# Two changes in the mixer of a two-layer decoder step: the prompt softmax works on scores that stay in PSUM, and the mixer's end runs in another order

## The reference, cut to what matters

```python
a = u @ w_in
y_c = silu(layernorm(depthwise_conv(a_conv))) @ pw      # 2 of the 8 row blocks of w_out
y_p = (window means - x) @ pool_w * pool_scale          # 2 blocks
y_a = sparse_attend(q, selected keys, selected values)  # 4 blocks
y = jnp.concatenate([y_c, y_p, y_a], axis=-1) @ w_out
```

```python
s = jnp.einsum('btngd,btknd->btngk', qg, ks) * HEAD_DIM ** -0.5
s = jnp.where(valid, s, -jnp.inf)
p = jax.nn.softmax(s, axis=-1)
o = jnp.einsum('btngk,btknd->btngd', p, vs)
```

## Time and profile before

| | us |
|---|---|
| median of 3 runs (lowest, highest) | 1151.5 (1150.71, 1151.86) |
| the profiled execution: its time | 1149.91 |
| its span in the trace | 1148.3 |
| busy: PE, DVE, ACT, GpSimd | 1082.8, 741.7, 514.2, 190.1 |

### The profile page before, as it was taken

How to read it: one execution, slowest core, us unless ns; L and a number is a source line. 1 busy time by engine, 2 the same in 40 slices (tenths; PEclk the granted TensorE clock), 3 DMA queues, 4 the chain that set the end, 5 groups by cost and what they waited for, 6 DMA issues and landing times.

```text
span 1148.3 us, 27626 instructions
## 1 busy us (share of the span) xinstructions
PE 1082.8 (94%) x9358; PEld 1025.1 (89%) x9358; DVE 741.7 (65%) x1211; ACT 514.2 (45%) x832; POOL 190.1 (17%) x241
## 2 busy tenths in 40 slices
PE   6999999999779999999999999999986799999996
PEld 6999999888448999999999999998863699999996
DVE  5676744788955766764476776448888466676544
ACT  5544433621444644443464444345215455444432
POOL 4211100411300311110041111004222022111001
PEclk9999999999879999999999999999998899999998
DMA  8464565343536355555435465563444445555541
GB/s 279 163 231 165 199 234 189 138 139 131 151 94 178 129 183 183 181 185 178 154 110 206 172 217 202 193 224 124 123 137 138 93 139 184 182 180 177 189 149 38
DMA packets 90465, 191.17 MB, mean 166 GB/s; under 512 B 12323, under 2 KB 48483, under 8 KB 90403
## 3 DMA queue, kind: packets, MB, share of 16 engines
q1 hardware_dynamic: 87426, 184.82, 48.7%
q0 software_dynamic: 2976, 5.53, 2.0%
HBM read 187.71 MB, written 2.59 MB: 166 GB/s over the span
## 4 chain that ended last, share of the span: by engine, by line
PE 85%; DVE 5%; ACT 3%; SPq 2%; issue 2%; DMA 1%; POOL 0%; DVEq 0%; POOLq 0%; ACTq 0%
PE PS L1105 23%; PE PS L1106 23%; PE PS L1107 23%; PE PS L1213 4%; SPq L263 2%; PE PS L1243 2%; PE PS L1141 2%; DVE w_lo L599 1%; PE PS L1153 1%; PE PS L1152 1%; PE PS L1156 1%; DVE rstd_post L628 1%; ACT w_hi L379 1%; PE PS L1454 1%; PE PS L1357 1%
## 5 line engine op out<-in xcount | busy, mean ns | idle before, releaser
L599 DVE TENSOR_TENSOR w_lo<-raw,w_hi 128x1024 fp32r<-128x1024 f32 x295 | 394.7, 1339 | 312.3 <-ACT w_hi L379 309.8
L379 ACT ACTIVATE w_hi<-raw 128x1024 fp32r<-128x1024 f32 x295 | 310.7, 1055 | 240.5 <-PE PS L1107 212.1
L1105 PE MATMUL PS<-x_hi,w_hi 128*128 128x264 f32 x1456 | 415.7, 286 | 0.7 <-DVE w_lo L599 0.6
L1106 PE MATMUL PS<-x_lo,w_hi 128*128 128x264 f32 x1456 | 412.5, 283 | 0.0
L1107 PE MATMUL PS<-x_hi,w_lo 128*128 128x264 f32 x1456 | 412.4, 283 | 0.0
L1105 PEld LDWEIGHTS PS<-x_hi,w_hi 128*128 128x128 f32 x1456 | 274.2, 188 | 2.3 <-DVE w_lo L599 1.6
L1106 PEld LDWEIGHTS PS<-x_lo,w_hi 128*128 128x128 f32 x1456 | 274.4, 188 | 0.1
L1107 PEld LDWEIGHTS PS<-x_hi,w_lo 128*128 128x128 f32 x1456 | 273.0, 187 | 0.0
L1105 PE MATMUL PS<-h_hi,w_hi 128*128 (+1 forms) x832 | 237.1, 285 | 3.4 <-issue 3.3
L1107 PE MATMUL PS<-h_hi,w_lo 128*128 (+1 forms) x832 | 236.9, 285 | 0.0
L1106 PE MATMUL PS<-h_lo,w_hi 128*128 (+1 forms) x832 | 236.2, 284 | 0.0
(11 more groups left out here) (255 smaller groups left out, 1000.2 us busy)
## 6 DMA issues: line engine op xcount, KB each, us to landing
raw<-in_wts SPq DMA_DIRECT2D x312, 512.0 KB, 3.6
kv<-in_kT SPq DMA_DIRECT2D x128, 64.0 KB, 2.0
kx<-in_kxT SPq DMA_DIRECT2D x128, 32.0 KB, 2.1
vx<-in_vC POOLq DMA_DIRECT2D x48, 64.0 KB, 2.5
raw<-in_vC SPq DMA_DIRECT2D x32, 64.0 KB, 2.3
kv<-in_vC SPq DMA_DIRECT2D x32, 64.0 KB, 1.9
out_yT<-h SPq DMA_DIRECT2D x8, 132.0 KB, 1.8
vx<-in_vC SPq DMA_DIRECT2D x16, 64.0 KB, 1.9
```

Source lines behind the costliest of these rows:

```text
L379: act.activation(w_hi[:, u % SPLIT, :], raw[:, u % RAW, :], ACT.Copy) \
L599: tt(w_lo[:, u % SPLIT, :], raw[:, u % RAW, :], w_hi[:, u % SPLIT, :].bitcast(F32), AL.subtract) \
L1105: pe.matmul(out, w_hi[:, w, cols], hi, start=start, stop=False)
L1106: pe.matmul(out, w_hi[:, w, cols], lo, start=False, stop=False)
```

## The change: what it does

**Masks on PE.** `scores(j)` now makes three float32 products for each part, which accumulate in PSUM: queries by keys, the new constant `hide` (the identity times -1e30) by the taken-or-not table `bias`, and the identity by the causal table in `con`. The scores stay in PSUM, in banks 2 and 3 for even pairs and 6 and 7 for odd ones (`SCORES`). DVE's L921 is gone: the maxima and the exponentials read PSUM, and the exponentials write `sp_`.

**Division in the transposing product.** DVE's two divisions of `sp_` become one 128x512 product that writes `share`, four identities scaled by the reciprocal sums. In the place of the transposes, PE multiplies `sp_` by `share`, which transposes and divides at once, but as float32 products. Both heads now use bank 0, so that head 1 waits for ACT's copy of head 0. The sample's `psm` gets the same treatment with `spread`; the 1025-wide division is gone.

**Order of the end.** The convolution's SiLU moves ahead of the third pair's last copy on ACT, and its product ahead of `dg`. The split of unit 18 moves ahead too. Output units 0, 1 and 2 begin with the row blocks 0 and 1 around the value products, and go on with blocks 2 and 3, then 4 to 7. The pooling's product stands behind the sample's transposes. The sample's value products share bank 3, and one copy (L561 of the changed kernel) takes the place of four.

```diff
+        SCORES = (2, 6)
 def exps(j):   # ACT
     act.wait_ge(sem["s_masked"], at_layer(L, "s_masked", j + 1))
+    if j >= 2:
+        act.wait_ge(sem["p_t"], at_layer(L, "p_t", 2 * j - 2))
...
-            t = sp_[:, j % 2, a, lo:hi]
-            ins = act.activation(t, t, ACT.Exp, scale=SCALE,
+            ins = act.activation(sp_[:, j % 2, a, lo:hi], PS[:, SCORES[j % 2] + a, lo:hi], ACT.Exp,
+                                 scale=SCALE,
...
-    act.activation(pT[:, a, :], PS[:, (7, 0)[a], 0:384], ACT.Copy).then_inc(sem["p_tc"], 1)
+    act.activation(pT[:, a, :], PS[:, 0, 0:384], ACT.Copy).then_inc(sem["p_tc"], 1)
...
+    if j == 2:
+        act.wait_ge(sem["c_norm"], at_layer(L, "c_norm", 1))
+        for c in range(2):
+            ins = act.activation(cacc[:, c, :], cacc[:, c, :], ACT.Silu,
...
+    warm(6, ACT.Exp)
 def masked(j):   # DVE
     dve.wait_ge(sem["s_p"], at_layer(L, "s_p", j + 1))
-    s = sp_[:, j % 2, :, :]
-    linked(stt(s, bias[:, :].unsqueeze(1).to_broadcast([128, 2, 384]), -BIG, PS[:, 2:4, 0:384],
-               AL.mult, AL.add))
+    s = PS[:, SCORES[j % 2]:SCORES[j % 2] + 2, :]
...
 def norm(j):   # DVE
     after(L, step(L, dve.reciprocal(sps[:, j % 2, :], sps[:, j % 2, :])))
-    for b, (lo, hi) in enumerate(((0, 256), (256, 384))):
-        t = sp_[:, j % 2, :, lo:hi]
-        ins = tt(t, t, sps[:, j % 2, b:4:2].unsqueeze(2).to_broadcast([128, 2, hi - lo]), AL.mult)
+    if j:
+        dve.wait_ge(sem["p_t"], at_layer(L, "p_t", 2 * j))
+    tt(share[:, :, :], ident.unsqueeze(1).to_broadcast([128, 4, 128]),
+       sps[:, j % 2, :].unsqueeze(2).to_broadcast([128, 4, 128]), AL.mult).then_inc(sem["p_norm"], 1)
 def scores(j):   # PE
     if j == 0:
+        pe.wait_ge(sem["mask_p"], at_layer(L, "mask_p", 1))
...
     else:
-        pe.wait_ge(sem["s_masked"], at_layer(L, "s_masked", j))
+        pe.wait_ge(sem["p_exp"], at_layer(L, "p_exp", j - 1))
     for a in range(2):
         rows = slice(64 * a, 64 * a + 64)
-        pe.matmul(PS[:, 2 + a, 0:256], aq[rows, j, 128:256], ak[rows, 0:256], start=True, stop=True)
-        ins = pe.matmul(PS[:, 2 + a, 256:384], aq[rows, j, 0:128], ak[rows, 0:128],
-                        start=True, stop=True)
+        for lo, n, q0, seen in ((0, 256, 128, C_CA1), (256, 128, 0, C_CA0)):
+            out = PS[:, SCORES[j % 2] + a, lo:lo + n]
+            pe.matmul(out, aq[rows, j, q0:q0 + 128], ak[rows, 0:n], start=True, stop=False)
+            pe.matmul(out, hide[:, :], bias[:, lo:lo + n], start=False, stop=False)
+            ins = pe.matmul(out, ident, con[:, seen:seen + n], start=False, stop=True)
...
-    ins = pe.transpose(PS[:, (7, 0)[a], 128 * n:128 * n + 128], p[:, c:c + 128], ident)
+    ins = pe.matmul(PS[:, 0, 128 * n:128 * n + 128], sp_[:, j % 2, a, c:c + 128],
+                    share[:, 2 * a + c // 256, :], start=True, stop=True)
...
+ out_part(0, (0, 1))            # PE, the mixer's end
  values(0)
...
  values(1)
+ out_part(1, (0, 1))
+ out_part(2, (0, 1))
...
+ pe.wait_ge(sem["pl_olo"], at_layer(L, "pl_olo", 1))
+ for o in range(SPLIT):
+     out_part(o, (2, 3))
+ pe.wait_ge(sem["o_slo"], at_layer(L, "o_slo", 1))
+ for o in range(SPLIT):
+     out_part(o, range(4, KD)).then_inc(sem["unit_done"], 1)
```

More of the change, by code:

```diff
@@ L485, in mixer @@
                 ins.then_inc(sem["conv_s"], 1)
-                for m in range(16, 18):
+                for m in range(16, 19):
                     split(L, u0 + m)
@@ L1014, in mixer @@
                 norm(3)
+                split(L, u0 + 18)
                 heads_out(2)
@@ L1050, in mixer @@
                 ins.then_inc(sem["o_ms"], 1)
+                dve.wait_ge(sem["pl_ohi"], at_layer(L, "pl_ohi", 1))
+                for c in range(2):
+                    ins = stt(h_lo[:, 2 + c, :], PS[:, 4 + c, 0:NT], pars[:, PSC + c:PSC + c + 1],
+                              h_hi[:, 2 + c, :].bitcast(F32), AL.mult, AL.subtract)
+                ins.then_inc(sem["pl_olo"], 1)
                 dve.wait_ge(sem["o_shi"], at_layer(L, "o_shi", 1))
@@ L1432, in mixer @@
                     ins.then_inc(sem["o_p"], 1)
+                raw_ready(pe, L, u0 + 15)
+                w = (u0 + 15) % RAW
+                pe.wait_ge(sem["c_silu"], at_layer(L, "c_silu", 1))
+                for c in range(2):
+                    for k in range(2):
+                        ins = pe.matmul(PS[:, 6 + c, 0:NT], raw[:, w, col(2 * k + c)], cacc[:, k, :],
+                                        start=(k == 0), stop=(k == 1))
+                ins.then_inc(sem["c_out"], 1)
                 pe.wait_ge(sem["dg"], at_layer(L, "dg", 1))
@@ L1435, in mixer, with out_part @@
                 for c in range(NPG):
-                    ins = pe.transpose(PS[:, 6 + c // 4, 128 * (c % 4):128 * (c % 4) + 128],
-                                       psm[:, 128 * c:128 * c + 128], ident)
+                    ins = pe.matmul(PS[:, 4 + c // 4, 128 * (c % 4):128 * (c % 4) + 128],
+                                    psm[:, 128 * c:128 * c + 128], spread[:, :], start=True, stop=True)
                 ins.then_inc(sem["p_st"], 1)
+                def out_part(o, ks):
+                    split_ready(L, u0 + N_IN + o)
+                    for k in ks:
+                        ins = three(PS[:, o, 0:NT], (u0 + N_IN + o) % SPLIT, col(k), h_hi[:, k, :], h_lo[:, k, :],
+                                    k == 0, k == KD - 1)
+                    return ins
+                pe.wait_ge(sem["c_olo"], at_layer(L, "c_olo", 1))
+                pe.wait_ge(sem["o_lo"], at_layer(L, "o_lo", 4))
+                out_part(0, (0, 1))
                 pe.wait_ge(sem["p_stc"], at_layer(L, "p_stc", 1))
```

118 lines of the change are left out of this document (44 added, 74 removed).

## The result

The changed kernel takes 1190.1 us (median of 4 runs, 1189.4 to 1197.0) against 1151.1 for the kernel before on the same chip: a ratio of 1.036, 95% interval 1.032 to 1.040, or +39 us. The forecast was +20 us and its range ended at 1182. The direction was right; the size was half of what came.

A forecast was written before the change was run, and what follows sets the result against it. It took DVE to set the pace up to the last AV, then a chain between engines, then PE alone; after the change PE. 78.9 us a layer, +14.4 us together, plus 2.8 a layer for clock: +20, 1171 us, range 1160 to 1182.

The forecast's parts named there:

- part A: Each layer from the first scores to the last AV: 42.4 us at full clock in layer 0, 13.4 more than before.
- the rest: Each layer from the last AV to the last output product: forecast 36.5 us.
- 12 records of 256 columns and 12 of 128, 2.6 + 1.45 = 4.1 us: One pair's group of scores with masks on PE, at full clock; 4.2 us with latency, 13.1 us more a layer.
- one or two falls a layer that each cost some 2 us of work on the path, 2.8 us a layer: PE's clock falls after waits in the mixer; added to the full-clock layout, it makes the forecast +20 us; chance 0.50.
- a wait forecast at 3.4 us: PE waits 3.4 us ahead of head 1's transposing product before scores(3), a place where the clock may fall.
- long low clock: Rival: two groups of scores and neighbours, some 12 us of PE work a layer, at half clock; 1179 us; chance 0.20.
- its gain buys idle time: Softmax stretch becomes a PE chain; DVE's gain of 6.0 us a layer only makes DVE wait.
- The one bank's wait: Head 1's transposing product waits for ACT's copy of head 0 out of the one bank; included in the layout.
- The transposing products: A product takes 0.24 us instead of a transpose's 0.12; with those for `psm`, 3.8 us more PE time a layer.
- The end: Between the last AV and the unbroken output products, the new order wins 5 us back a layer.
- faster: Rival: mask products priced near transposes fit in PE's waits, group 2.3 us, layer 4.8 us shorter; 1142 us; chance 0.05.
- no change on balance: Rival: PE's waits in the softmax stretch are all filled and the end wins 4 to 5 us; 1151 us; chance 0.05.

The follow-up runs named there:

- e6: The changed kernel with float32 products that add no result put into two PE waits (pair 1's second transposing product, the sample's first): 1179.4 us.
- e12: e2 with float32 products that add no result put into four PE waits around the first parts of the softmax and four products ahead of `dg`: 1172.1 us.
- e2: The changed kernel with the division back on DVE and transposes back on PE, still in one bank, masks staying on PE: 1202.8 us.
- e10: e3 with both heads' transposes in one bank, so head 1's wait for the copy of head 0; transposes and divisions as before: 1150.8 us.
- e9: e3 with the division in the transposing product: DVE writes `share`, PE multiplies by it, each head keeps its own bank: 1140.7 us.
- e3: The kernel before with only the new order of the end, including the sample's product by `spread`: 1141.9 us.
- e7: The changed kernel with the mask as one bfloat16 product of 384 columns for each head, behind adjacent query products of both heads: 1151.9 us.
- e1: The changed kernel with the masks alone undone: DVE adds a ready table and copies the scores to SBUF, where ACT reads them: 1154.6 us.
- e5: The changed kernel with one float32 mask product for each part instead of two, by a table that holds both masks: 1187.3 us.
- e4: The changed kernel with queries and keys over all rows as operands of both mask products, same shapes and count, so masks are left out: 1190.7 us.

## Why the prediction was wrong

The forecast put a layer at 78.9 us at full clock (42.4 for part A, 36.5 for the rest) and 2.8 us on top for the clock. At full clock the changed kernel's part A takes 46.9 (e6), and the rest 36.45 (e12, the same program there but for four added products), together 83.4. The two layers took 92.6 and 90.6. So of the 20 us missed, some 9 are terms at full clock and some 11 the clock; that is an estimate, which takes layer 1 at full clock to be as long as layer 0.

**The step that failed first: "12 records of 256 columns and 12 of 128, 2.6 + 1.45 = 4.1 us".** The count was right, the prices weren't: 0.265 and 0.163 us for a record in a group of 5.46 us, not 0.22 and 0.12 (the first product of each three takes some 0.1 us more still). I had the 0.22 from a row of the chain of waits. An entry there runs from where the entry ahead of it ended (374.80) to its own end (375.25); in PE's timeline the same product starts at 374.64. The chain shows what lies on the path, cut to length, and not what an instruction takes. The timeline had the price of products in a row, in layer 0 of the kernel before:

```profile
300.72 1.16 PE L1379 MATMUL PS<-cacc,con 128*128 128x264 f32 x4
...
374.64 0.61 PE L1141 MATMUL PS<-sq,con 128*128 128x264 f32 x2
```

Four records in 1.16 us, some 0.1 of it latency, is 0.26 us for each. With that price the group would have come out at 4.7 us. The rest couldn't be read there: the 0.12 us came from transposes, and no row that I read had a full-height float32 product of 128 columns. The error weighs 1.26 us a group, 5.0 a layer; part A at full clock is 4.5 us longer than laid out (46.9 against 42.4).

**The step that failed worse: "one or two falls a layer that each cost some 2 us of work on the path, 2.8 us a layer".** The place and the cause of the fall were right (a wait forecast at 3.4 us, found as 3.04), and so was the count: two falls in each layer. The length was taken from the earlier trace rows as if the clock came back soon once PE works. It stayed low for 20.5 and 13.7 us, over a whole group of scores and more. The low stretch in part A of layer 0 cost 7.7 us, not 2; over both layers the clock cost some 16 us instead of 5.6. An us at the low clock cost 0.38 us (7.7 for 20.5, changed against e6) and 0.40 (34.0 for the 85 us less in the stretch, e2 against e12). The rival "long low clock" had this mechanism, with a chance of 0.20 and 13 us for both layers; with the 9 us of prices on top it would have given 1188. It should have been the forecast: I argued against it that a group of scores fills 4 us, where the length of the group is what the low clock doubles.

**Right:** DVE no longer sets the pace and its gain buys idle time (5.33 us of waiting ahead of the maxima). The one bank's wait was in the layout; e10 puts it at 8.9 us, so a term that I had spread over the whole was a main one. The transposing products cost nothing on balance where DVE sets the pace (e9); where PE does, they cost some 1.7 us a layer (part A of e6 against e12). The end: 5 us a layer forecast, 8 in all by e3. The rivals "faster" and "no change on balance" rested on cheap mask products; e7 shows that they can be had, by another type, at 1.29 us a group and 1151.9 us.

The parts, from medians: the end's order -8, the share product -1, the one bank +9, what e1 has beyond these (scores in two pairs of banks, two more DVE instructions for the mask table, product and one bank together) +5, float32 masks +35.5. Each is the step from one kernel to the next, so the one bank's 9 us are its price beside cheap scores; beside the float32 masks no run has it. The eight groups are 4.5 us longer each than the earlier trace rows has them, 36 us of PE time. What PE fills of its waits by that and what the clock adds weigh against each other, and DVE's eight passes of 0.95 us less bring nothing, since DVE then waits for the scores (4.8 to 9.3 us ahead of each pair's maxima in layer 0).

**Open:** what decides whether the clock comes back after 3.4 us or after 20. In these runs every stretch above 10.2 us but one (13.7 us in e10) lies over float32 groups with mask products. Nor is it known what decides whether it falls: with the same waits of 1.23 and 0.92 us in pair 0 it stayed full in both layers of the changed kernel, and fell in layer 0 of e5 and in layer 1 of e6 and e7. With transposes in the place of products (e2 against the changed kernel, the waits 0.27 and 0.33 us longer in pair 0) the low clock grew from 54 to 91 us over all executions, and e3 has 36 where e9 with products has 22. The Trainium skill says in the same page, Part 4, that transposes don't count as busy work in the way products do; both pairs of kernels fit that. But the waits differ between them too, and e12 has the transposes and hardly any low clock, so a part of the transposes in it isn't shown.

## What to carry to other kernels

Price a product by a row where several stand one behind the other, from start to start, at the operand type, width and height that the new code has, and with the order of heights that it has; a single product at the end of a chain is no price. Where a wait of 2 to 3 us stands ahead of long products, price those at half clock as well and let the forecast's range hold that case; a few idle products in the wait are a cheap test, and here they gave back 11 and 31 us. A mask that holds only zeros, ones and twos went through PE as one bfloat16 product for each head, behind query products that stand next to each other, and the group took a quarter of its time (1.29 us instead of 5.46). What shares a PSUM bank between two heads puts everything that stands on ACT ahead of the copy in PE's path (3.04 us of waiting here).

## What the runs showed of the hardware

- A granted clock of 0.50 lasted 20.5 and 13.7 us in the changed kernel, with PE busy without a break for 14.2 and 12.5 us of them, and 37.5 us in e2 with waits of 3.08 and 1.65 us in it.
- The same wait of 3.04 us was followed by 20.5 and 13.7 us (changed kernel) or 3.4 us (e7) of low clock.
- The low clock differs between executions of one kernel: 38 to 74 us in the four of e4. With next to none in the mixers (e12) the four lie within 1 us.
- Products added in waits made kernels faster by 10.7 us (e6) and 30.7 us (e12).
- Query products of two heads on different halves of the rows overlap when they are adjacent (eight records in 0.92 us, e7), and don't with a full-height product between them (0.60 us each for two records).
- Three float32 products of 128 columns took 0.94 us, three transposes 0.55, in the same place (changed kernel and e12).
